# Second block's mixers: projection units of half the contraction by 512 columns, in place of the whole contraction by 256

## What is computed

```python
def mixer_sublayer(x, n1, w_in_l, qg, kg, rpb_l, og, w_out_l, tables):
    h = rms_norm_2(x, n1)
    proj = h @ w_in_l                                  # 1024 -> 2560 columns
    qa, ka, va, qd, kd, vd, qc, kc, vc = jnp.split(proj, cuts, axis=-1)
    qa, ka = rms_norm_2(heads(qa, H_NA), qg[0]), rms_norm_2(heads(ka, H_NA), kg[0])
    out_a = neighbourhood_attention(qa, ka, heads(va, H_NA), rpb_l, na_idx, na_dr, na_dc)
    qd = partial_rotary(rms_norm_2(heads(qd, H_DIL), qg[1]), cos1, sin1)     # kd alike
    out_d = dilated_window_attention(qd, kd, heads(vd, H_DIL), dil_idx, dil_val)
    qc = axial_rotary(rms_norm_2(heads(qc, H_GQ), qg[2]), cos_r, sin_r, cos_c, sin_c)   # kc alike
    out_c = gqa_block_attention(qc, kc, vc)
    mix = concatenate([rms_norm_2(out_a, og_a), rms_norm_2(out_d, og_d), rms_norm_2(out_c, og_c)])
    return x + mix @ w_out_l
```

## Time and profile before

| what | value |
|---|---|
| runs | 1653.95, 1654.03, 1659.03 us |
| the profiled execution's span | 1654.3 us, and the page gives no time around it |
| PE, PEld | 99%, 85% of the span |
| DVE, ACT, POOL | 69%, 55%, 7% |
| the chain that ended last, by engine | PE 91%, DVE 4%, ACT 3% |
| first layer's mixer, projection to norm of the FFN | 1031.5 to 1154 us |
| second layer's mixer | 1343.2 to 1463.6 us |
| a weight load of 1 MB, median from issue to landing | 4.9 us |

### The profile page before, as it was taken

The page is one execution under the profiler, slowest core; times in us unless marked ns, Lnnn a source line. Parts: engine busy times, 40 slices in busy tenths (PEclk is TensorE's granted clock), DMA queues, the critical chain, the costliest instruction groups (busy, mean ns, idle before and its releaser), DMA issues.

```text
span 1654.3 us, 25690 instructions
## 1 busy us (share of the span) xinstructions
PE 1631.8 (99%) x9727; PEld 1400.4 (85%) x9727; DVE 1148.5 (69%) x1626; ACT 917.0 (55%) x1470; POOL 116.4 (7%) x130
## 2 busy tenths in 40 slices
PE   8999999999999999999999999999999999999999
PEld 7888897888888888898688888887888899788887
DVE  6766656666667666679866666887777778677776
ACT  6444566544455444536754455775655567655554
POOL 0000011000001000042000000140000003010000
PEclk9999999999999999999999999999999999999999
DMA  8555451555555555532145554442555554245552
GB/s 285 194 193 180 151 202 52 199 211 198 180 177 181 197 180 188 183 138 79 52 168 198 181 186 169 154 128 103 198 184 187 193 174 133 102 153 189 178 194 99
DMA packets 42670, 276.78 MB, mean 167 GB/s; under 512 B 7121, under 2 KB 8034, under 8 KB 9826
## 3 DMA queue, kind: packets, MB, share of 16 engines
q1 hardware_dynamic: 40882, 271.00, 46.9%
q0 software_dynamic: 1712, 4.73, 1.3%
HBM read 274.66 MB, written 1.05 MB: 167 GB/s over the span
## 4 chain that ended last, share of the span: by engine, by line
PE 91%; DVE 4%; ACT 3%; issue 1%; POOL 1%; DMA 0%; POOLq 0%; SPq 0%; ACTq 0%; DVEq 0%
PE bank L830 28%; PE bank L848 22%; PE bank L831 14%; PE bank L731 3%; PE bank L979 2%; PE bank L687 2%; PE bank L689 2%; PE bank L688 2%; PE bank L980 2%; PE bank L981 2%; DVE w_lo L1937 1%; PE bank L1014 1%; PE bank L1051 1%; PE bank L1031 1%; POOL x_rstd L2590 1%
## 5 line engine op out<-in xcount | busy, mean ns | idle before, releaser
L830 PE MATMUL bank<-xt_both,w_hi 128*128 128x512 f32 x2016 | 709.4, 396 | 0.5 <-DVE QT L2170 0.5
L1937 DVE TENSOR_TENSOR w_lo<-raw,w_hi 128x2048 fp32r<-128x2048 f32 (+1 forms) x254 | 580.3, 2286 | 169.7 <-ACT w_hi L1455 168.1
L831 PE MATMUL bank<-xt_both,w_lo 128*128 128x256 f32 x2016 | 562.6, 279 | 0.0
L1455 ACT ACTIVATE w_hi<-raw 128x2048 fp32r<-128x2048 f32 (+1 forms) x254 | 484.9, 1910 | 56.4 <-PE bank L689 35.1
L830 PEld LDWEIGHTS bank<-xt_both,w_hi 128*128 128x128 f32 x2016 | 378.5, 188 | 91.4 <-DVE w_lo L1937 0.8
L831 PEld LDWEIGHTS bank<-xt_both,w_lo 128*128 128x128 f32 x2016 | 379.7, 188 | 2.3
L1679 ACT ACTIVATE KT<-bank 128x256 f32<-128x256 f32 x264 | 86.9, 381 | 336.3 <-PE bank L831 332.3
L848 PE MATMUL bank<-w_hi,h_lo 128*128 128x512 f32 x528 | 208.2, 394 | 0.0
L848 PE MATMUL bank<-w_hi,h_hi 128*128 128x512 f32 x528 | 208.2, 394 | 0.0
L848 PE MATMUL bank<-w_lo,h_hi 128*128 128x512 f32 x528 | 208.2, 394 | 0.0
L848 PEld LDWEIGHTS bank<-w_hi,h_hi 128*128 128x128 f32 x528 | 99.4, 188 | 23.6 <-issue 0.5
(11 more groups left out here) (357 smaller groups left out, 2201.0 us busy)
## 6 DMA issues: line engine op xcount, KB each, us to landing
raw<-in_stream SPq DMA_DIRECT2D x254, 1024.0 KB, 4.9
work<-in_rpb POOLq DMA_DIRECT2D x32, 64.0 KB, 6.1
X<-in_x SPq DMA_DIRECT2D x2, 512.0 KB, 5.1
raw<-in_stream SPq DMA_DIRECT2D x2, 512.0 KB, 6.1
prob<-in_cmp_w POOLq DMA_DIRECT2D x1, 1024.0 KB, 7.7
O<-in_cmp_w POOLq DMA_DIRECT2D x1, 1024.0 KB, 13.0
out<-X SPq DMA_DIRECT2D x4, 256.0 KB, 2.0
cst<-in_consts SPq DMA_DIRECT2D x1, 712.0 KB, 10.0
```

The source lines that it names most:

```text
L830: pe.matmul(both, w_hi[:, sl, cols], xt_both[:, :, k, :], start=(k == 0), stop=False)
L831: ins = pe.matmul(dst[:, 0:S], w_lo[:, sl, cols], xt_hi[:, k, :], start=False, stop=(k == KD - 1))
L1455: act.activation(to, src, ACT.Copy).then_inc(hi_done, 1)
L1937: dve.tensor_tensor(to, src, hi.bitcast(F32), ALU.subtract).then_inc(lo_done, 1)
```

## The change

A block is now 512 columns (`b = c // 2`), and unit `c` is half of the contraction (`c % 2`, four rows of 128) by these 512 columns. The stream on the host isn't changed: `half_rows` on SP loads unit `c` with two DMAs of 512 KB, one from each of two neighbouring units, with a semaphore more for the first (`first_in`). `part(c, t)` takes the place of `half`: 12 matmuls of 512 columns into a whole bank for one token tile; `first_part` takes that of `first_block`. A block ends with its odd unit, one token tile after the other, and each end counts `pj_ps`; `evac(c)` now copies one token tile of a block, 512 columns, in one instruction. After an odd unit PE waits for its own `pj_ps` and then counts the unit as used. On ACT `evac(4)` moves behind `tiles(1)`, `head_squares(1)` behind `evac(5)`, `evac(6)` and `evac(8)` behind `pair_out(0)` and `pair_out(2)`. On DVE `head_sums(1)` moves behind `split(u0 + 7)`. The loads of all other units stay in loops on SP. The diff, with unchanged lines cut:

```diff
@@ -73,9 +73,10 @@
-SEC_KINDS = ((QC, 8, 0, 1, 384), (QD, 12, 8, 4, 384), (QA, 8, 20, 7, 256))
+SEC_KINDS = ((QC, 8, 0, 1, 384), (QD, 12, 8, 5, 384), (QA, 8, 20, 7, 256))
 SEC_S, SEC_T, SEC_O = (4, 5), 6, 7
-SEC_PROJ_BANK = (0, 1, 2, 3) + (0, 1) * 3
+SEC_PROJ_BANK = (0, 6, 2, 3) + (0, 1) * 3
+SEC_UNITS = 10
 GRID = 64
...
@@ -303,6 +304,7 @@
         raw_in = [sem(f"raw_in{i}") for i in range(NRAW)]
+        first_in = [sem(f"first_in{i}") for i in range(NRAW)]
         hi_done, lo_done = sem("hi_done"), sem("lo_done")
...
@@ -318,7 +320,7 @@
         fc_in, fg_done = sem("fc_in"), sem("fg_done")
-        pj_evac = sem("pj_evac")
+        pj_evac, pj_ps = sem("pj_evac"), sem("pj_ps")
         ft_ready_d, ft_ready_p = sem("ft_ready_d"), sem("ft_ready_p")
...
@@ -356,6 +358,8 @@
+        SEC_PARTS = [U[f"sec_in{l}"] + c for l in range(2) for c in range(SEC_UNITS)]
+
...
@@ -635,14 +639,37 @@
             next_load(8)
-            turns = N_UNITS // NRAW
-            with sp.Fori(3, turns) as i:
-                for j in range(NRAW):
-
-                    sp.wait_ge(lo_done, i * NRAW + (j - NRAW + 1))
-                    load(i * NRAW + j, j)
-            for u in range(turns * NRAW, N_UNITS):
-                next_load(u)
+
+            def whole_units(lo, hi):
+
+                first, end = -(-lo // NRAW), hi // NRAW
+                for u in range(lo, first * NRAW):
+                    next_load(u)
+                with sp.Fori(first, end) as i:
+                    for j in range(NRAW):
+
+                        sp.wait_ge(lo_done, i * NRAW + (j - NRAW + 1))
+                        load(i * NRAW + j, j)
+                for u in range(end * NRAW, hi):
+                    next_load(u)
+
+            def half_rows(u0, c):
+
+                j, b, kk = (u0 + c) % NRAW, c // 2, c % 2
+                sp.wait_ge(lo_done, u0 + c - NRAW + 1)
+                to = raw[:, j, :].rearrange("p (k h n) -> p h k n", h=2, n=256)
+                for h, landed in ((0, first_in[j]), (1, raw_in[j])):
+                    src = stream[u0 + 2 * b + h][:, kk * 1024:(kk + 1) * 1024].rearrange("p (k n) -> p k n", n=256)
+                    sp.dma_start(to[:, h], src).then_inc(landed, 16)
+
+            at = 9
+            for l in range(2):
+                u0 = U[f"sec_in{l}"]
+                whole_units(at, u0)
+                for c in range(SEC_UNITS):
+                    half_rows(u0, c)
+                at = u0 + SEC_UNITS
+            whole_units(at, N_UNITS)
             for j in range(4):
...
@@ -965,22 +992,50 @@
-                def half(c, t, k0=0, k1=KD):
+                def part(c, t, k0=0, k1=KD // 2):
...
                         pe.wait_ge(lo_done, u0 + c + 1)
-                        if c >= 4:
-                            pe.wait_ge(pj_evac, p0 + (c - 3 if c < 6 else c - 1))
+                    if c % 2 == 0 and c >= 4:
+                        pe.wait_ge(pj_evac, p0 + (t + 1 if c == 4 else c - 2 + t + 1))
                     sl = (u0 + c) % NSPLIT
-                    dst = bank[SEC_PROJ_BANK[c]][:, t * 256:(t + 1) * 256]
+                    dst = bank[SEC_PROJ_BANK[c // 2 * 2 + t]][:, :]
                     tok = slice(t * P, (t + 1) * P)
-                    for k in range(k0, k1):
-                        cols = slice(k * 256, (k + 1) * 256)
+                    for j in range(k0, k1):
+                        k = c % 2 * (KD // 2) + j
+                        cols = slice(j * 512, (j + 1) * 512)
                         pe.matmul(dst, xt_hi[:, k, tok], w_hi[:, sl, cols], start=(k == 0), stop=False)
...
                         ins = pe.matmul(dst, xt_lo[:, k, tok], w_hi[:, sl, cols], start=False, stop=(k == KD - 1))
-                    if t == 1 and k1 == KD:
+                    if c % 2 and k1 == KD // 2:
+                        ins.then_inc(pj_ps, 1)
+                    elif t == 1 and k1 == KD // 2:
                         ins.then_inc(unit_used, 1)
+                    if c % 2 and t == 1 and k1 == KD // 2:
+                        pe.wait_ge(pj_ps, SEC_UNITS * l + c + 1)
+                        pe.sem_inc(unit_used, 1)
+
+                def first_part():
+
+                    sl = u0 % NSPLIT
+                    pe.wait_ge(lo_done, u0 + 1)
+                    for k in range(KD // 2):
+                        pe.wait_ge(xth, 8 * turn + k + 1)
+                        cols = slice(k * 512, (k + 1) * 512)
+                        for t in range(NT):
+                            dst = bank[SEC_PROJ_BANK[t]][:, :]
+                            tok = slice(t * P, (t + 1) * P)
+                            pe.matmul(dst, xt_hi[:, k, tok], w_hi[:, sl, cols], start=(k == 0), stop=False)
+                            pe.matmul(dst, xt_hi[:, k, tok], w_lo[:, sl, cols], start=False, stop=False)
+                    for k in range(KD // 2):
+                        pe.wait_ge(xtl, 8 * turn + k + 1)
+                        cols = slice(k * 512, (k + 1) * 512)
+                        for t in range(NT):
+                            dst = bank[SEC_PROJ_BANK[t]][:, :]
+                            tok = slice(t * P, (t + 1) * P)
+                            ins = pe.matmul(dst, xt_lo[:, k, tok], w_hi[:, sl, cols], start=False, stop=False)
+                    ins.then_inc(unit_used, 1)
+                    pe.wait_ge(xtl, 8 * turn + KD)
...
@@ -1042,8 +1097,6 @@
                     if m == 3:
-                        pe.wait_ge(pj_evac, p0 + 9)
-                    if m == 6:
                         pe.wait_ge(pj_evac, p0 + 10)
...
@@ -1110,50 +1163,52 @@
-                first_block(u0, bank[SEC_PROJ_BANK[0]], turn)
-                for c in range(1, 5):
-                    half(c, 0)
-                    half(c, 1)
+                first_part()
+                part(1, 0)
+                part(1, 1)
+                for c in range(2, 5):
+                    part(c, 0)
+                    part(c, 1)
                 transposes(0)
                 transposes(1)
-                half(5, 0)
+                part(5, 0)
                 scores(0)
-                half(5, 1)
+                part(5, 1)
...
                 turn_p(0)
-                half(6, 0)
+                part(6, 0)
                 turn_p(1)
-                half(6, 1)
+                part(6, 1)
...
                 values(0)
-                half(7, 0)
+                part(7, 0)
                 turn_p(3)
-                half(7, 1, 0, 2)
+                part(7, 1, 0, 1)
                 transposes(2)
                 transposes(3)
-                half(7, 1, 2, 5)
+                part(7, 1, 1, 3)
                 transposes(4)
-                half(7, 1, 5, KD)
+                part(7, 1, 3, 4)
...
                 values(1)
-                half(8, 0)
+                part(8, 0)
                 turn_p(5)
-                half(8, 1)
+                part(8, 1)
...
                 values(2)
-                half(9, 0)
+                part(9, 0)
                 turn_p(7)
...
                 square_sums(0)
-                half(9, 1)
+                part(9, 1)
...
@@ -1449,6 +1504,8 @@
                 act.wait_ge(raw_in[sl], on(16 * (u // NRAW + 1), 32, i))
+                if i is None and u in SEC_PARTS:
+                    act.wait_ge(first_in[sl], 16 * (1 + [n for n in SEC_PARTS if n % NRAW == sl].index(u)))
                 if u >= NSPLIT:
...
@@ -1520,14 +1577,13 @@
-                    act.wait_ge(unit_used, u0 + c + 1)
+                    b, t = c // 2, c % 2
+                    act.wait_ge(pj_ps, SEC_UNITS * l + c + 1)
                     r = rms_turn(6 + 2 * l)
...
                         act.wait_ge(rstd_done, r + 1)
-                    for t in range(NT):
-                        ins = act.activation(proj[:, t, c * 256:(c + 1) * 256],
-                                             bank[SEC_PROJ_BANK[c]][:, t * 256:(t + 1) * 256], ACT.Copy, scale=x_rstd[:, r, t:t + 1])
-                    ins.then_inc(pj_evac, 1)
+                    act.activation(proj[:, t, b * 512:(b + 1) * 512], bank[SEC_PROJ_BANK[c]][:, :], ACT.Copy,
+                                   scale=x_rstd[:, r, t:t + 1]).then_inc(pj_evac, 1)
...
@@ -1602,25 +1658,25 @@
                 split(u0 + 6)
-                evac(4)
                 tiles(0)
                 tiles(1)
-                head_squares(1)
+                evac(4)
                 exponentials(0)
...
                 evac(5)
+                head_squares(1)
...
                 split(u0 + 8)
-                evac(6)
                 split(u0 + 9)
...
                 pair_out(0)
+                evac(6)
                 tiles(2)
...
@@ -1632,13 +1688,13 @@
                 pair_out(1)
-                evac(8)
                 split(u0 + 11)
...
                 pair_out(2)
+                evac(8)
                 tiles(5)
...
@@ -2093,11 +2149,11 @@
                 maxima(0)
-                head_sums(1)
...
                 split(u0 + 7)
+                head_sums(1)
...
```

## The result

The changed kernel took 1667.22 us (median of 6 runs, 1665.04 to 1667.77), the kernel before 1654.8 beside it (6 runs, 1653.78 to 1659.52). The ratio is 1.0067, with a 95% interval from 1.0056 to 1.0079: some 11 us slower. The forecast was 1662.6 within 1657.0 to 1666.0, counted from 1654.0 for the kernel before: 8.6 us more, within 3 and 12. Direction and mechanism are as forecast, the size was too small. By the ratio the change costs 11.1 us, near the upper end of the range; the medians are 12.4 apart, and the new median itself lies 1.2 us above 1666.0. The profiled execution's span is 1665.3 us against 1654.3.

A forecast was written before the change was run, and what follows sets the result against it. PE, busy 99% of the span, was taken as the bound, with DVE's chain setting the pace before the first layer's first scores. 1654.0 + 7.1 (both layers' waits) + 1.5 (clock) = 1662.6 us, range 1657.0 to 1666.0.

The forecast's parts named there:

- Squares behind block 2, root exposed: Dilated heads in both mixers: later squares expose POOL's 4.16 us root, third transposes 3.5 us later, about 3.5 a layer.
- First scores: Head of each mixer's chain: first scores come 0.5 us earlier in the first layer, 0.6 in the second.
- From the transposes to the fourth scores: Third transposes to fourth scores: 3.55 us becomes 3.7, with 0.07 less for matmuls and one own wait added.
- Own waits: PE waits for its own last matmul at odd parts, five a layer: 0.25 us each, up to 2.5 for ten.
- the matmuls' gain: Mixer projections: 240 matmuls of 512 columns replace 480 of 256, saving 1.9 us a layer if nothing else holds PE.
- Loads, evictions' places, turned block: Split loads, later evac(2) and evac(4), first turned block about 1.3 us later on ACT: all costed at nothing.
- PE's clock: Mixers: PE's new idle waits of some 4 us bring one fall to 1.2 GHz more in total, +1.5 us.
- a fall in each layer: Rival: PE, idle 4 us, falls to 1.2 GHz both times, losing 1.5 us in each layer: 1664.1 us; chance 0.12.
- The wait 20% shorter and no fall: Condition given for the range's lower end, 1657.0 us: shorter wait for the root, no added clock fall.
- the half-exposed root: Rival: POOL's root only half on the path, 2 us less a layer: 1657.1, or 1658.6 with a fall; chance 0.09.
- two falls and the wait 15% longer: Condition given for the range's upper end, 1666.0 us: two clock falls and a longer wait for the root.

The follow-up runs named there:

- e1: Kernel before, with only the moves of the dilated heads' squares (ACT) and sum (DVE) to their later places: 1667.76 us, ratio 1.0073.
- e2: Changed kernel, POOL's root of the dilated heads made in two instructions, one per token tile, each preparation waiting for its own: 1659.0 us, ratio 1.0022.
- e5: Changed kernel, with squares, sums and root of 8 of the 12 dilated heads a token tile made early: 1655.66 us, ratio 1.0004.
- e4: Changed kernel without PE's waits for its own end behind odd units: 1667.68 us, ratio 1.0074.
- e10: e8 with PE's waits for its own end put back: 1654.97 us, ratio 0.9995.
- e8: Changed kernel with early heads as in e5, whole-unit loads, no own waits, half of part(7, 1) ahead of the third transposes: 1655.01 us, ratio 0.9993.
- e9: e8 with 8 unread 512-column matmuls in PE's wait ahead of the first layer's first transposes: 1653.04 us, ratio 0.9988.
- e6: Changed kernel, with the stream laid out on the host so one 1 MB DMA in 8 KB pieces loads a unit: 1665.29 us, ratio 1.0058.
- e7: Changed kernel, with 16 unread 512-column matmuls in PE's wait ahead of the third transposes, first layer only: 1666.67 us, ratio 1.0062.

## Why the prediction was right in kind and too small in size

- **Squares behind block 2, root exposed: right.** From the second layer's first scores, the forecast had the mean squares 10.3 us later, the preparation 14.85, the third transposes 22.85. The trace has 10.7 (1392.54), 15.0 and 22.94. Root 4.17 and DVE's wait 2.8 as forecast. e1, e2 and e5 show that this is what costs: put alone into the kernel before it gives the loss, shortened it gives back the same time, and taken off the path it leaves no loss.
- **First scores: half the forecast.** 0.28 and 0.43 earlier instead of 0.5 and 0.6. That makes the transposes 3.9 and 3.75 later instead of 3.5. A part of it is the evictions: one of 512 columns takes 0.69 to 0.70 us, where I took 0.62 from another 512-column copy, so the two at the head give 0.3, not 0.5.
- **From the transposes to the fourth scores: 0.2 short.** I put 3.7 us; at full clock it is 3.92 (in the second layer of e2, 1399.60 to 1403.52, and of e5, 1395.36 to 1399.29).
- **Own waits: right, or a little high.** Counted at 0.25 each, 2.5 in all; e4 puts the ten at 2.3, and e10 at 1.8 against e8 and 1.1 against e9. As forecast, this leaves little of the matmuls' gain.
- **Loads, evictions' places, turned block: right at nothing** (e6).
- **PE's clock: the term that was too small.** The prediction said "I count one fall more in total, +1.5". There are two new ones, one behind each wait, each 6.8 us long instead of 3.4, while the old one is gone. Against the 3.92 us at full clock they cost 6.55 - 3.92 = 2.6 and 6.23 - 3.92 = 2.3 us. Less the old 1.5 that is 3.4 net, not 1.5. The price of a short fall was right: where one of 3.4 us followed the same wait, the stretch took 5.52 (e2, first layer), 5.37 and 5.52 (e6) and 5.45 us (e7), 1.45 to 1.6 over 3.92. Two such falls less the old one would have been the +1.5 of the forecast. What it had wrong is their length, which it took from the one fall in the rows. The rival "a fall in each layer" had the place right and the length too short in the same way.
- **That 1.5 is the right price was luck: its working does not give it.** 19 matmuls where 28 would have run at 0.120 us is 9 x 0.120 = 1.1 us. The two layers of the kernel before give the true price: from the fourth scores to the transposes behind the mixer the second took 64.85 us, with the fall, and the first 63.40, without: 1.45.
- **The range's ends do not follow from their conditions.** The wait 20% shorter and no fall would be about 1659.6, not 1657.0, which is the half-exposed root; two falls and the wait 15% longer about 1665.3, not 1666.0.

At full clock the first layer loses 3.93 + 0.37 - 0.19 = 4.1 us and the second 3.75 + 0.37 - 0.2 = 3.9 (the wait; 3.92 for the 3.55 of before; what comes back behind the fourth scores, without the old fall): 8.0 where I had 7.1. So 8.0 + 3.4 - 0.5 (ahead and behind) = 11 where the forecast had 8.6. The medians say the same with more weight on the clock: with the clock taken off they are 7.6 us apart (1658.6 and 1651.0), and the clock's part is 8.3 against 3.3, 5.0 more. The kernel before's profile had three falls where most of its runs, at 0.998, lost only two falls' worth. A part of that is chance: the fall at 277 us in its profile is missing in the changed kernel's, but there again in those of e6, e8 and e10.

The Trainium skill ("TensorE: Matmul & The Clock Gate", what's actually happening) holds idle time to be what closes the gate. The rows agree, as all nine waits of about 4 us that PE spent idle were followed by a fall and none of the three that it spent working; e2's second layer shows a wait of 2.37 us without one, and e7 a fall after 1.43 and 1.30 us.

## What to carry to other kernels

When a tiling change moves the moment at which the last column of a group is complete, follow everything computed from that group, down to the smallest instruction on the slowest engine: here a root of 24 elements a partition on POOL, once nothing lay beside it, cost more than 240 matmuls fewer a layer gave back. Split such a step so that only what really comes late is made late. When PE, at 99%, gets a wait of some microseconds, price the clock behind it too: here 3.4 to 5.0 us on top of 8. And remember that speeding up the work ahead of a fixed point only lengthens the rest, and can lose by it what it gained (e4, e8).

## What the runs showed of the hardware

- **POOL's root is paid by the element.** 128x24 took 4.17 us, 128x16 2.90, 128x8 1.65 (at 273.67 in the changed kernel's trace), two of 128x12 together 4.50, and 128x2 0.70: 0.156 us an element of a partition and about 0.4.
- **A root that starts while DVE's low part runs waits for it.** The low part reads two tiles in SBUF and writes a third. In the changed kernel's trace, DVE's low part, then on POOL a root of two elements beside it and one with nothing beside it:

```profile
1036.79 2.29 DVE L1993 TENSOR_TENSOR w_lo<-raw,w_hi 128x2048 fp32r<-128x2048 f32 x1
```
```profile
1036.97 2.70 POOL L2646 TENSOR_TENSOR x_rstd<-ms,neg_half 128x2 f32<-128x2 f32 x1 [184.50 <-DVE ms L2002]
1044.49 0.70 POOL L2646 TENSOR_TENSOR x_rstd<-ms,neg_half 128x2 f32<-128x2 f32 x1 [4.83 <-DVE ms L2002]
```

  In the twelve profiles 156 roots of 128x2 started while a low part ran, and all took 2.67 to 2.70 us; the other 48 took 0.69 to 0.71. The roots of 128x8 took 3.61 beside it (8, in e5, e8, e9 and e10) and 1.65 without (12). They end 0.6 and 1.5 us after the low part (1039.08 in the rows above, 1077.20 in e5), which is nearly their whole time alone, and the low part takes its usual 2.29. It matters who starts first: 24 roots of 128x16 in which the low part started only after them took 2.92, and 8 without it 2.90. The Trainium skill ("GPSIMD Engine Reference", specifications) has POOL share its SBUF interfaces with DVE, with contention from instructions of two SBUF inputs; these rows agree. No run moved a low part away from a root, so this rests on what the traces have side by side.
- **A fall may last 3.4 or 6.8 us at the same place, behind the same wait.** The falls behind the two waits lasted 6.8 us in the changed kernel's profile and 3.4 in e6's, with waits equal to 0.04 us and the same order of PE's work. They began between 1.85 us before the wait's end (changed kernel, second layer) and 1.4 us after it (e1, first layer).
- **The clock goes with most of the spread between runs.** Of the kernel before, 23 runs beside the last experiments took 1653.62 to 1661.54 us at mean clocks of 0.999 to 0.994; the slowest six had 0.996 or less, and the others 0.997 or more. With the clock taken off, the spread of 7.9 us is 3.1.
